# Compression in a hybrid attention block: one product for the values with four copies by ScalarE, and an earlier chain for the compressed keys

## What is computed

```python
def compress(t, pe, w1, w2):
    c = t.reshape(B, n_chunk, CMP_STRIDE, G, Dh)
    blocks = jnp.concatenate([c[:, :-1], c[:, 1:]], axis=2) + pe[None, None, :, None, :]
    flat = blocks.transpose(0, 1, 3, 2, 4).reshape(B, n_cmp, G, CMP_BLOCK * Dh)
    return jax.nn.silu(flat @ w1) @ w2

k_cmp = rms_norm(compress(kv[:, :, 0, 0], cmp_pe[0], cmp_w1[0], cmp_w2[0]), k_gain[0])
v_cmp = compress(kv[:, :, 0, 1], cmp_pe[1], cmp_w1[1], cmp_w2[1])
```

## Time and profile before

| what | value |
|---|---|
| median of 3 runs | 746.54 us (746.1 to 749.1) |
| the profiled execution's own time | 745.74 us |
| its span in the trace | 743.7 us |
| PE busy | 698.9 us (94%) |
| VectorE busy | 366.8 us (49%) |
| ScalarE busy | 291.8 us (39%) |
| GpSimd busy | 103.5 us (14%) |

### The profile page before, as it was taken

How to read it: one execution, slowest core, us unless ns; L and a number is a source line. 1 busy time by engine, 2 the same in 40 slices (tenths; PEclk the granted TensorE clock), 3 DMA queues, 4 the chain that set the end, 5 groups by cost and what they waited for, 6 DMA issues and landing times.

```text
span 743.7 us, 9977 instructions
## 1 busy us (share of the span) xinstructions
PE 698.9 (94%) x3703; PEld 595.9 (80%) x3703; DVE 366.8 (49%) x713; ACT 291.8 (39%) x630; POOL 103.5 (14%) x152
## 2 busy tenths in 40 slices
PE   7995989999989789979799999999999999999998
PEld 5984768888879778868679888888888888888886
DVE  5557556546696653575675544412324454532311
ACT  5564545346485342354534434321122433422110
POOL 2444642310050300223110000000000000000000
PEclk9999899999999979999999999999999999999999
DMA  7341133111053100010003332232322323232302
GB/s 273 124 143 46 43 94 107 33 57 30 4 159 123 57 1 1 2 58 28 29 28 115 114 100 99 87 112 85 114 85 92 106 85 113 85 114 85 100 1 99
DMA packets 17953, 60.04 MB, mean 81 GB/s; under 512 B 2120, under 2 KB 2248, under 8 KB 17906
## 3 DMA queue, kind: packets, MB, share of 16 engines
q1 hardware_dynamic: 16562, 55.41, 22.4%
q0 software_dynamic: 1200, 3.94, 1.7%
q10 hardware_dynamic: 144, 0.07, 0.0%
HBM read 57.26 MB, written 2.15 MB: 80 GB/s over the span
## 4 chain that ended last, share of the span: by engine, by line
PE 84%; DVE 7%; ACT 3%; issue 3%; POOL 1%; DMA 1%; SPq 0%; DVEq 0%; ACTq 0%; POOLq 0%
PE bank L1397 14%; PE bank L1399 14%; PE bank L1398 14%; PE bank L1695 8%; PE bank L1697 8%; PE bank L1696 8%; PE bank L1418 6%; PE bank L1581 5%; PE bank L1544 2%; PE bank L1623 1%; DVE w_lo L906 1%; ACT p_buf L720 1%; PE bank L1555 1%; DVE s_buf L1062 1%; DMA x<-x 1%
## 5 line engine op out<-in xcount | busy, mean ns | idle before, releaser
L906 DVE TENSOR_TENSOR w_lo<-raw,w_hi 128x1024 fp32r<-128x1024 f32 (+3 forms) x97 | 112.5, 1166 | 128.6 <-ACT w_hi L598 128.4
L598 ACT ACTIVATE w_hi<-raw 128x1024 fp32r<-128x1024 f32 (+3 forms) x97 | 97.4, 1011 | 120.2 <-PE bank L1399 118.2
L1695 PE MATMUL bank<-act_hi,w_hi 128*128 128x512 f32 (+3 forms) x288 | 106.9, 371 | 0.0
L1697 PE MATMUL bank<-act_hi,w_lo 128*128 128x512 f32 (+3 forms) x288 | 106.8, 371 | 0.0
L1696 PE MATMUL bank<-act_lo,w_hi 128*128 128x512 f32 (+3 forms) x288 | 106.8, 371 | 0.0
L1397 PE MATMUL bank<-w_hi,a_hi 128*128 128x512 f32 x256 | 99.7, 389 | 0.0
L1399 PE MATMUL bank<-w_hi,a_lo 128*128 128x512 f32 x256 | 99.7, 389 | 0.0
L1398 PE MATMUL bank<-w_lo,a_hi 128*128 128x512 f32 x256 | 99.7, 389 | 0.0
L1397 PE MATMUL bank<-w_hi,act_hi 128*128 128x512 f32 (+3 forms) x224 | 92.4, 413 | 2.3 <-DVE act_lo L919 2.3
L1399 PE MATMUL bank<-w_hi,act_lo 128*128 128x512 f32 (+3 forms) x224 | 81.6, 364 | 0.0
L1398 PE MATMUL bank<-w_lo,act_hi 128*128 128x512 f32 (+3 forms) x224 | 81.4, 363 | 0.0
(11 more groups left out here) (192 smaller groups left out, 1086.9 us busy)
## 6 DMA issues: line engine op xcount, KB each, us to landing
raw<-weights SPq DMA_DIRECT2D x86, 512.0 KB, 3.3
raw<-weights SPq DMA_DIRECT2D x7, 384.0 KB, 4.4
x<-x SPq DMA_DIRECT2D x4, 512.0 KB, 6.5
bias<-bias_by_distance POOLq DMA_DIRECT2D x1, 2048.0 KB, 9.5
y<-x SPq DMA_DIRECT2D x8, 256.0 KB, 2.2
raw<-weights SPq DMA_DIRECT2D x4, 288.0 KB, 2.8
raw<-weights SPq DMA_DIRECT2D x4, 280.0 KB, 3.1
consts<-consts SPq DMA_DIRECT2D x1, 688.0 KB, 4.2
```

The costliest lines, as they stand in the source:

```text
L598: act.activation(w_hi[:, m % RING, 0:width], raw[:, n % RAW, 0:width], ACT.Copy).then_inc(*hi_done.mark(n))
L906: dve.tensor_tensor(w_lo[:, m % RING, 0:width], raw[:, n % RAW, 0:width], w_hi[:, m % RING, 0:width].bitcast(F32), ALU.subtract).then_inc( ...
L1695: pe.matmul(dst, h[:, ws], act_hi[:, k, cols], start=k == 0, stop=False)
L1697: ins = pe.matmul(dst, l[:, ws], act_hi[:, k, cols], start=False, stop=k == KD - 1)
```

## The change

The values' activation moves from u 21 to u 20 and makes one product of 62 columns (written over the exponential), and ScalarE copies it four times into `hid_v` at u 21 with one instruction. The keys' chain moves up: kc from u 21 to u 18, its squares from 22 to 19, the scaling from 26 to 21, the transpose from 27 to 22, the copies from 28 to 23. vc moves from u 23 to 24 on PE and from 24 to 25 on VectorE. In GpSimd's order the keys' power comes after two of the four MLA rows, and the branch sum of win 3 after all of them.

```diff
             pool.wait_ge(*gaing_in.at())
-            for t in range(NT):
-                mix_row_of(0, t)
-            sum_branches("win", 3)
+            mix_row_of(0, 0)
+            mix_row_of(0, 1)
             pool.wait_ge(*dve_step.at("kc_ss"))
             rsqrt("kc", kc_rs[0:64, :], kc_ss[0:64, :], HD)
+            mix_row_of(0, 2)
+            mix_row_of(0, 3)
+            sum_branches("win", 3)
             sum_branches("win", 2)
@@ scalar
+                if u == 21:
+                    act.wait_ge(*dve_step.at("hid_v"))
+                    act.activation(hid_v[:, :, :, 0:N_CMP], z_buf[:, 1, 1, :].rearrange("p (g c) -> p g c", g=2).unsqueeze(2).to_broadcast([P, 2, 4, N_CMP]),
+                                   ACT.Copy).then_inc(*exp_small.mark("hid_v"))
@@ vector, compress(u)
-                if u in (16, 21):
-                    kv = (u - 16) // 5
+                if u in (16, 20):
+                    kv = (u - 16) // 4
...
                     else:
-                        for g in range(2):
-                            rep = lambda v: v[:, g, :].unsqueeze(1).to_broadcast([P, 4, N_CMP])
-                            dve.tensor_tensor(hid_v[:, g, :, 0:N_CMP], rep(z), rep(r), ALU.mult).then_inc(*dve_step.mark(("hid_v", g)))
+                        dve.tensor_tensor(e, z_buf[:, 0, kv, :], z_buf[:, 2, kv, :], ALU.mult).then_inc(*dve_step.mark("hid_v"))
                 if u in (21, 23, 25, 27):
                     mix_lows(0, (u - 21) // 2)
-                if u == 22:
+                if u == 19:
                     dve.wait_ge(*turned.at("kc"))
...
-                if u == 24:
+                if u == 25:
                     dve.wait_ge(*turned.at("vc"))
...
-                if u == 26:
+                if u == 21:
                     dve.wait_ge(*rsqrt_done.at("kc"))
...
-                if u == 28:
+                if u == 23:
                     dve.wait_ge(*turned.at("kcT"))
@@ tensor, compress(u)
-                if u == 21:
+                if u == 18:
                     pe.wait_ge(*dve_step.at("hid_k"))
...
-                if u == 23:
-                    pe.wait_ge(*dve_step.at(("hid_v", 1)))
+                if u == 24:
+                    pe.wait_ge(*exp_small.at("hid_v"))
...
-                if u == 27:
+                if u == 22:
                     pe.wait_ge(*dve_step.at("kc2"))
                     turn("kcT", [kc_sq], (dve_step, "k_cmp"))
```

## The result

The changed kernel takes 750.93 us (median of 17 runs, 748.79 to 753.62) against 746.54 us before (17 runs, 745.26 to 750.01). The ratio is 1.0051, with a 95% interval of 1.0036 to 1.0067: slower by about 0.5%, where 744.9 us and a small gain were forecast, and outside the range of 741.0 to 747.6 us.

What follows compares the result with a forecast made beforehand. PE bounds the kernel (84% of the chain), losing time idle or at low clock. The orders tie at full clock; low clock of 4.5 less 2.9 gives 1.6 us won: 746.54 - 1.6 = 744.9 us, range 741.0 to 747.6.

Steps and rivals of the forecast that it cites:

- values' activation: VectorE: 2.63 us of two products removed, one product added, 0.22 us undisturbed; ScalarE's copy costed at nothing.
- the handoffs: Between engines: 0.04 us from PE to L1062, 0.11 us from PE to L1072, 0.14 us from VectorE to PE.
- the meeting with GpSimd: Product asked for at 255.15, GpSimd's L553 from 255.00: product ends at 256.42, not 255.37; scaling waits for row 3's L553.
- the product gets in first: Rival: product precedes GpSimd's L553, shortening the u 22 stall; 742.2 us, or 740.5 if the clock never falls; chance 0.25.
- The other stalls: PE stalls after the first, before the transposes at u 23 and u 25: about 1.2 and 2.15 us.
- The two orders level at full clock: Start of the output projection at full clock: 274.35 in the new order, 274.3 in the old, so no gain by itself.
- I take 3.4 us low after the first ... and 3.4 us after the third: 2.9 us: TensorE's low clock after the new first and third stalls: 1.2 and 1.7 us lost, 2.9 us in all.
- The bounds: Limits on the clock term: 3.3 us won if the third stall spares the clock; nothing won if the first costs 6.8.
- the forecast's own range: Run time of the main forecast case, 742.7 to 747.3 us, with about 0.8 us of spread between runs; chance 0.55.
- The low clock of the old order: Before the output projection: 5.8/2 + 3.6 x 0.47 = 4.5 us lost to TensorE's low clock.
- The rival "slower": First stall lowers the clock, two following keep it low until u 28; projection starts at 285, 753 us; chance 0.05.
- a microsecond that reaches 278.87 sooner should be kept by what follows: After the first output projection: PE busy all of 21.00 us after 279 at full clock, so time won earlier is kept.

Runs made afterwards that it cites:

- filler at u 22 alone: Changed kernel plus 16 unread identity transposes on TensorE before the wait for the scaled keys at u 22; ratio 0.9984 to the kernel before.
- two later stalls filled: Changed kernel plus unread identity transposes on TensorE at u 23 and u 25 only, first stall left open; ratio 0.9954 to the kernel before.
- shifted kernel before: Kernel before plus 22 identity transposes on TensorE at the end of u 27; ratio 1.0062 to the kernel before.
- values' part alone: Kernel before with one values' product of 62 columns at u 21 and ScalarE's four copies at u 22, keys unmoved; ratio 0.9957.
- pair of kernels with filler: Kernel before with unread transposes in its three stalls, 0.9951; the same with the single values' product and ScalarE's copies added, 0.9911.
- GpSimd held: Changed kernel with one more GpSimd wait, for the values' product before scaling MLA row 2; ratio 1.0023 to the kernel before.

## Why the prediction was wrong

- *The values' activation, the handoffs, the meeting with GpSimd.* Right. The product was to take 1.27 us and took 1.31; the scaling was to be held by the second L553 and was, 0.90 us long. PE's first idle was to be 2.83 us and was 2.81, with 0.25 behind it for the 0.34 forecast. ScalarE's copy took 0.42 us and held nothing up. The product started 0.04 us after L553, where the sum had 0.15 (it took 0.78 us from L551 to L553, and the earlier trace rows have 0.82); the meeting was as close as the case "the product gets in first" feared.
- *The other stalls.* 1.2 and 2.15 us were forecast at full clock. At full clock they are 1.22 and 2.26 us (PE's brackets before units 21 and 23 with filler at u 22 alone). At low clock PE's own work fills a part of them, 0.80 and 1.65 us.
- *The two orders level at full clock.* Right: 274.35 against 274.3 forecast, 26.43 against 26.25 us of stage measured.
- *The step that failed: "I take 3.4 us low after the first ... and 3.4 us after the third: 2.9 us".* It took 20.5 us of low clock and cost 6.6 us. I priced each stall by the row of a single stall of its length, one at a time. With the two later stalls filled the clock was back after 7 us in the new order; with them open (0.80 us at 264.95, 1.65 us at 273.55) it did not come back until PE was nearly through u 26 to 28. The bounds (nothing to 3.3 us won) had no end on the losing side for that reason; the forecast's own range, written as 742.7 to 747.3, begins at 742.4 by its terms. The low clock of the old order, 4.5 us in the sum, was right at 4.4 us (its terms add up to 4.6).
- *What stays open in that step.* I leaned on one profile of the old order, in which the clock came back at 265.9 after PE had worked without a gap (5.78 us busy of 5.80). In the second profile of the same kernel PE worked without a gap between stalls of 4.08 and 1.90 us too, and the clock stayed at 1.2 GHz from 260.8 to 274.5, 13.7 us in one piece. So unbroken work of this length did not always bring it back, and one profile was too little to price a stall from.
- *The rival "slower"* named this mechanism and its place, at a chance of 0.05 and a price of 11 us, which is PE's whole work doubled. The price was too high. PE's work from kcT to the projection took 18.9 us where 11 us were reckoned at full clock and 22 at half: a unit without a stall takes 2.56 us at low clock (275.36 to 277.92) for 1.35, and the clock was back 1.6 us before the projection. The stalls shrank from 3.7 to 2.7 us besides. The chance was far too low.
- *The second step that failed: "a microsecond that reaches 278.87 sooner should be kept by what follows"*, read as a rule for both signs. 2.66 us later at the projection became 5.07 us at 400 us, because two stretches of low clock behind the stage no longer lay beside a wait. The shifted kernel before shows this with nothing changed but the 22 transposes in front of the projection.

Why the clock fell in 320 to 390 us at all was not studied. What sets when it falls and when it comes back was not isolated, and neither was why the values' part alone won 3.2 us where the shorter wait is worth 1.3 us. An earlier start against the low stretches behind may be the reason, as in the pair of kernels with filler above; it was not tried by itself.

## What to carry to other kernels

Do not price TensorE's stalls one by one, nor by their sum: the changed kernel's were shorter together than the old one's (5.5 us against 7.3) but stood closer together, and had 20.5 us of low clock for 10 to 14. Take more than one profile before a stretch of low clock is priced, since the same kernel showed 10 us in one and 14 us in another. Before an order is judged by its time, put work that nobody reads into its stalls, in a bank that is free; that run tells what the order is worth without the clock, and it may be the faster kernel. Look at what GpSimd runs beside a VectorE instruction with two inputs in SBUF, since one wait of 1.1 us there was over a third of a stall (with GpSimd held the first stall was 1.82 us for 2.81).

## What was not expected of the hardware

Extra matmuls made both kernels faster: 44 transposes more in the changed one win 1.1%, 63 more in the old one 0.5%. With stalls of no more than 1.1 us each, 2.7 us in sum within 13 us, the granted clock stood at 1.2 GHz for 19 us of the stage in one execution (748.62 us), while the three fastest runs of the same kernel leave some 2 to 5 us for it by the estimate above. In the changed kernel PE's records cover 5.91 of the 6.00 us from 266 to 272 while the clock stays there: busy records alone did not bring it back at once. And a stage that was 2.3 us longer cost 4.6 us of run time (1.0062, interval 1.0045 to 1.0080).
